# Block 0's top-k moved into its w_q products, nine weight buffers in the first phase, and a new pace in the second

## The reference

```python
x = x + mixed @ w_out                      # mixed: window attention (8 heads) and retention (8 heads) of RMSNorm(x) @ w_in
q = (h @ w_q).reshape(PEER_BLOCK, 8, 2, 128)            # h = RMSNorm(x), in blocks of 128 frames
s = einsum('thcd,hcnd->thcn', q, sub_keys)              # 16 rows of 128 scores per frame
sv, si = top_k(s, 16)
cand = sv[:, :, 0, :, None] + sv[:, :, 1, None, :]      # 8 x 256 candidates, and their indices
top_s, pos = top_k(cand, 16); expert = take(cidx, pos); g = softmax(top_s)
hid = gelu(einsum('thkd,td->thk', u_table[expert], h))
x = x + einsum('thk,thkd->td', g * hid, v_table[expert])
y = RMSNorm(x)
```

## Time and profile before

| | us |
|---|---|
| median of 3 runs | 3667.43 |
| lowest and highest | 3660.72, 3675.81 |
| profiled execution, its time | 3681.99 |
| profiled execution, its span | 3679.9 |

### The profile page before, as it was taken

How to read it: one execution, slowest core, us unless ns; L and a number is a source line. 1 busy time by engine, 2 the same in 40 slices (tenths; PEclk the granted TensorE clock), 3 DMA queues, 4 the chain that set the end, 5 groups by cost and what they waited for, 6 DMA issues and landing times.

```text
span 3679.9 us, 27703 instructions
## 1 busy us (share of the span) xinstructions
PE 1964.1 (53%) x9448; PEld 1081.0 (29%) x9448; DVE 2036.5 (55%) x4571; ACT 323.7 (9%) x778; POOL 2104.6 (57%) x2183
## 2 busy tenths in 40 slices
PE   7976615665673347655833357565723333333446
PEld 6765511543440115433601024233401000000001
DVE  2378486467539673564476853654586744443220
ACT  2211101011110010110100010101100000000000
POOL 0034345566456675566466665665576666666665
PEclk9986866886895668767956579778856555556669
DMA  6587877999999999999998999999999999999998
GB/s 222 178 294 277 308 231 290 357 399 342 358 388 364 362 350 395 399 362 395 362 385 328 360 366 394 400 364 402 346 355 370 365 374 366 366 367 376 377 365 323
DMA packets 442170, 1286.15 MB, mean 350 GB/s; under 512 B 39408, under 2 KB 157936, under 8 KB 442032
## 3 DMA queue, kind: packets, MB, share of 16 engines
q0 software_dynamic: 313344, 1140.99, 81.7%
q1 hardware_dynamic: 126224, 134.48, 11.0%
q10 hardware_dynamic: 2464, 8.91, 0.6%
HBM read 1274.50 MB, written 9.44 MB: 349 GB/s over the span
## 4 chain that ended last, share of the span: by engine, by line
POOL 22%; another core or an unknown queue 14%; DMA 12%; issue 11%; PE 8%; DVE 5%; ACT 0%; ACTq 0%; POOLq 0%; SPq 0%
POOL ring L629 22%; DMA ring<-in_peer_v_dram,v_idx 8%; PE ps L1255 4%; PE ps L1214 4%; DMA ring<-in_peer_u_dram,u_idx 3%; DVE ring L897 3%; DMA wbuf<-in_peer_w_q_dram 1%; DVE work L974 0%; DVE work L970 0%; PE ps L1413 0%; DVE work L979 0%; DMA out_dram<-x_v 0%; PE ps L1362 0%; DVE work L1071 0%
## 5 line engine op out<-in xcount | busy, mean ns | idle before, releaser
L897 DVE CUSTOM_DVE_ANT_0 ring<-ring,ps 128x1024 f32<-128x1024 f32 x1088 | 1302.2, 1218 | 975.5 <-DMA ring<-in_peer_u_dram,u_idx 855.4
L629 POOL DMA_INDIRECT ring<-in_peer_u_dram,u_idx x1088 | 1044.5, 960 | 1061.5 <-issue 275.9
L1214 PE MATMUL ps<-ring,spread 128*32 128x512 f32 x4352 | 876.5, 910 | 1241.3 <-DMA ring<-in_peer_v_dram,v_idx 1084.9
L629 POOL DMA_INDIRECT ring<-in_peer_v_dram,v_idx x1088 | 1058.3, 973 | 495.2 <-issue 304.1
L1255 PE MATMUL ps<-wbuf,actT 128*128 128x256 f32 (+1 forms) x2944 | 703.0, 399 | 105.9 <-issue 89.0
L1214 PEld LDWEIGHTS ps<-ring,spread 128*32 128x32 f32 x4352 | 178.1, 143 | 1833.5 <-issue 1765.7
L1255 PEld LDWEIGHTS ps<-wbuf,actT 128*128 128x128 f32 (+1 forms) x2944 | 559.6, 193 | 274.4 <-issue 174.7
L970 DVE MAX8 work<-work 128x8 f32<-128x128 f32 (+3 forms) x432 | 110.8, 322 | 129.9 <-ACT work L866 119.9
L974 DVE FIND_INDEX8 work<-work 128x8 uint32<-128x128 f32 (+3 forms) x432 | 134.0, 329 | 4.9 <-issue 4.7
L699 ACT COPY spread<-weightT 128x16 f32<-128x16 f32 x64 | 14.0, 219 | 894.8 <-remote 713.7
L897 DVE DVE_READ_ACCUMULATOR2_ANT hidden<- 128x1 f32 x1088 | 89.7, 82 | 0.2 <-issue 0.2
(11 more groups left out here) (153 smaller groups left out, 1271.8 us busy)
## 6 DMA issues: line engine op xcount, KB each, us to landing
wbuf<-in_w_in_dram SPq DMA_DIRECT2D x55, 1024.0 KB
wbuf<-in_peer_w_q_dram SPq DMA_DIRECT2D x40, 1024.0 KB
wbuf<-in_w_out_dram SPq DMA_DIRECT2D x20, 1024.0 KB
ring<-in_peer_u_dram,u_idx POOLq DMA_INDIRECT x1088
ring<-in_peer_v_dram,v_idx POOLq DMA_INDIRECT x1088
x_v<-x_scratch ACTq DMA_DIRECT2D x8, 512.0 KB
out_dram<-x_v ACTq DMA_DIRECT2D x8, 512.0 KB
x_in<-in_x_prompt_dram SPq DMA_DIRECT2D x7, 512.0 KB
```

Of the source, the lines that this page charges most:

```text
L629: pool.indirect_dma_start(ring[:, at % RING, :], None, table, bass.IndirectOffsetOnAxis(ap=idx, axis=0)).then_inc(landed[at % RING], 16)
L897: ch.put(v_.tensor_tensor_reduce(out=row, in0=row, in1=ux_ps, scale=1.0, scalar=0.0, op0=ALU.mult, op1=ALU.add, accum_out=hidden[:, k:k + ...
L1214: mm = pe.matmul(ps[j:j + 32, B_ACC + c, :], spread[:, at:at + 32], tile[:, 512 * c:512 * c + 512], start=(t % 32 == 0), stop=(t % 32 == 3 ...
```

## The change

Phase 0 gets nine weight buffers: the three of `wbuf`, two in `wide`, four in ring places 5 to 12. SyncE issues all 23 pieces of block 0 in one row, each when the piece nine before it has been used, and only then the x loads of blocks 1 and 2, then the store of block 0's x. The first half of the query transposes goes behind w_q product 4, its score products behind product 5, their copies with them; the h transposes go behind products 2 and 6. The second half's score products go between piece 0 and piece 1 of the early projection, and for block 0 both halves use banks 0 and 1. The copy of block 0's row into PSUM (`load`) moves from the list of phase 1 to ScalarE's work ahead of the copies of piece 1. TensorE's transpose of the expert numbers comes after four pieces of the early projection instead of eight. GpSimd's first gather also waits for the four query copies. `BEGUN_PEER` = 58 takes the place of 105 for phase 1, so its total is 346: the slot of norm2 and w_q rises, and all 128 U rows stand ahead of the top-k steps.

```diff
+WFIRST = 9
-    NORM, PIECE, ATTN, PEER = 6, 3.6, 55, 105
+    NORM, PIECE, ATTN, PEER, BEGUN_PEER = 6, 3.6, 55, 105, 58
...
-                            ("w_q", g * N_Q * self.PIECE), ("peer", g * self.PEER)):
+                            ("w_q", g * N_Q * self.PIECE),
+                            ("peer", g * (self.BEGUN_PEER if begun else self.PEER))):
...
+        wfirst = ([wbuf[:, i] for i in range(WRING)]
+                  + [wide[:, i * KC * WCOLS:(i + 1) * KC * WCOLS].rearrange("p (k n) -> p k n", k=KC) for i in range(2)]
+                  + [ring[:, i:i + 2, :].rearrange("p r (k n) -> p (r k) n", n=WCOLS) for i in (5, 7, 9, 11)])
...
-                m = n - WRING
+                m = n - (WRING if b0 else WFIRST)
...
@@ block.sync @@
-                    stream(blocks, range(N_IN))
+                    for n in range(PIECES):
+                        load_piece(blocks, n)
                     for b in following:
                         load_x(b)
-                    stream(blocks, range(N_IN, PIECES))
+                    sp.wait_ge(x1_ready, N_OUT)
+                    sp.dma_start(x1_dram[0, :, :], x_of[0]).then_inc(x1_stored[place(0)], 16)
                     stream(following, range(EARLY_LOADS))
@@ block.gpsimd @@
                     if b == 0 and k == 0:
                         pool.wait_ge(first_experts, 1)
                         pool.wait_ge(x1_stored[place(0)], 16)
+                        pool.wait_ge(pqT_ready, 4)
@@ block.scalar @@
-                        if b == 0 and m in early_h:
-                            h_copied(early_h[m], following[early_h[m]])
+                        if b == 0 and m == 2:
+                            h_copied(0, following[0])
+                        if b == 0 and m in (4, 7):
+                            pq_copied(b, 2 * (m // 7), P)
+                        if b == 0 and m == 5:
+                            sims_copied(b, 0, P)
+                        if b == 0 and m == 6:
+                            h_copied(1, following[1])
...
-                    if b == 0:
-                        projected(following, range(EARLY - 2))
+                    else:
+                        projected(following, range(1))
+                        sims_copied(b, 2, T)
+                        load(b)
+                        projected(following, range(1, 4))
                     th.step("peer", g, 0.85)
                     act.wait_ge(gdiff_ready, b + 1)
...
-                        projected(following, range(EARLY - 2, EARLY))
+                        projected(following, range(4, EARLY))
@@ block.vector @@
-                    dve.wait_ge(sims_ready, 4 * b + 4)
+                    dve.wait_ge(sims_ready, 4 * b + 4 if b else 2)
...
+                        if b == 0 and h0:
+                            dve.wait_ge(sims_ready, 4)
@@ block.tensor @@
-                        if b == 0 and m in early_h:
-                            h_transposed(early_h[m], following[early_h[m]], h2T_ready, 2)
+                        if b == 0 and m == 2:
+                            h_transposed(0, following[0], h2T_ready, 2)
+                        if b == 0 and m == 4:
+                            pe.wait_ge(hT_ready, 2 * (following[0] + 1))
+                            pq_transposed(b, 0, P)
+                        if b == 0 and m == 5:
+                            similar(b, 0, P)
+                        if b == 0 and m == 6:
+                            h_transposed(1, following[1], sims_ready, 2)
...
+                    else:
+                        pe.wait_ge(hT_ready, 2 * (following[1] + 1))
+                        pq_transposed(b, 2, T)
+                        project(following, grp + 1, range(1))
+                        similar(b, 2, T)
                     if b == 0:
-                        pe.wait_ge(sims_ready, 4)
-                        project(following, grp + 1, range(EARLY))
+                        project(following, grp + 1, range(1, 4))
                     th.step("peer", g, 0.95)
                     pe.wait_ge(expert_ready, 2 * b + 1)
                     transposed(0, T, lambda c: expert_f[0:T, :], 1, expert_tr)
+                    if b == 0:
+                        project(following, grp + 1, range(4, EARLY))
```

More of the change, by code:

```diff
@@ L675, in item, with load @@
                     spread_out(b, k)
[L676 to L682, removed]
+                elif kind == "load" and b:
+                    load(b)
                 elif kind == "final":
                     final(b)
+            def load(b):
+                act.wait_ge(h2_ready, b + 1)
+                if b == SAMPLE:
+                    act.wait_ge(sample_packed, 48)
+                ch.settle()
+                ch.put(copy(ux_ps, u_x[:, b % UXBUF, :]), ux_ready)
             def spread_out(v, piece):
@@ L741, in h_copied, with q_bank, pq_copied, sims_copied @@
                     ch.put(copy(act_of[b][:, 4 * i:4 * i + 4, 0:T], four(i, T)), hT_ready)
+            def q_bank(b, i):
+                return i % 2 if b == 0 else i
+            def pq_copied(b, first, T):
+                for i in (first, first + 1):
+                    act.wait_ge(pq_tr, 4 * b + i + 1)
+                    ch.put(copy(pqT[:, 4 * i:4 * i + 4, 0:T], four(q_bank(b, i), T)), pqT_ready)
+            def sims_copied(b, first, T):
+                for i in (first, first + 1):
+                    act.wait_ge(sims_done, 4 * b + i + 1)
+                    ch.put(copy(sims[0:T, 4 * i:4 * i + 4, :], four(q_bank(b, i), P)[0:T]), sims_ready)
             def projected(blocks, pieces):
@@ L860, in _ @@
                         act.wait_ge(expert_ready, 2 * b)
[L861 to L866, removed]
-                    if b == 0:
-                        projected(following, range(EARLY - 2))
+                        for i in (0, 2):
+                            pq_copied(b, i, T)
+                        for i in (0, 2):
+                            sims_copied(b, i, T)
+                    else:
+                        projected(following, range(1))
+                        sims_copied(b, 2, T)
+                        load(b)
+                        projected(following, range(1, 4))
                     th.step("peer", g, 0.85)
@@ L1234, in h_transposed, with q_bank, pq_transposed, similar @@
                     transposed(i, T, lambda c: h_nat[0:T, (4 * i + c) * P:(4 * i + c + 1) * P], 4, h_tr)
+            def q_bank(b, i):
+                return i % 2 if b == 0 else i
+            def pq_transposed(b, first, T):
+                pe.wait_ge(q_ready, N_Q * b + 2 * (first + 2) if b == 0 else N_Q * (b0 + G))
+                for i in (first, first + 1):
+                    transposed(q_bank(b, i), T, lambda c: pq_of[b][0:T, (4 * i + c) * P:(4 * i + c + 1) * P], 4, pq_tr)
+            def similar(b, first, T):
+                for i in (first, first + 1):
+                    pe.wait_ge(pqT_ready, 4 * b + (first + 2 if b == 0 else 4))
+                    for c in range(4 * i, 4 * i + 4):
+                        mm = pe.matmul(ps[0:T, q_bank(b, i), (c % 4) * P:(c % 4 + 1) * P], pqT[:, c, 0:T],
+                                       keysT[:, c, :], start=True, stop=True)
+                    mm.then_inc(sims_done, 1)
             def project(blocks, grp, pieces):
@@ L1401, in _ @@
                     th.step("peer", g)
-                    pe.wait_ge(q_ready, N_Q * (b0 + G))
-                    pe.wait_ge(h2T_ready, 2 * (b0 + G))
-                    if b == 0:
[L1405 to L1417, removed]
-                        pe.wait_ge(sims_ready, 4)
-                        project(following, grp + 1, range(EARLY))
+                    if b:
+                        pe.wait_ge(h2T_ready, 2 * (b0 + G))
+                        pe.wait_ge(q_ready, N_Q * (b0 + G))
+                        if g:
+                            pe.wait_ge(sims_ready, 4 * b)
+                            pe.wait_ge(expertT_ready, b)
+                        for i in (0, 2):
+                            pq_transposed(b, i, T)
+                        for i in (0, 2):
+                            similar(b, i, T)
+                    else:
[3 more added lines that the diff above has]
+                        similar(b, 2, T)
+                    if b == 0:
+                        project(following, grp + 1, range(1, 4))
                     th.step("peer", g, 0.95)
```

21 lines of the change are left out of this document (15 added, 6 removed).

## The result

The changed kernel takes 3693.85 us (median of 8 runs, 3681.21 to 3700.87), the kernel before 3677.15 beside it (3660.72 to 3686.69, 8 runs). The ratio is 1.0053, 95% interval 1.0029 to 1.0076: by that ratio 19.5 us slower (the two medians differ by 16.7), where +1.4 was forecast. A second set of runs gave 1.0055 (1.0034 to 1.0077). The profiled execution took 3694.40, its span is 3692.2.

The account below looks back on a forecast made before the run. Taken as bound by transfers with DMA full, the change being worth the shift in block 2's top-k end (634.5 us): +16.8 + 11.4 + 5 + 2 - 28 - 5.8 = +1.4, so 3669 us, range 3640 to 3692.

Parts of the forecast that it names:

- part 2: Block 0's early projection: 14 products remain behind the wait for the second indices, ending 258.7 against 241.9; +16.8 us.
- part 3: Second phase: dots move ahead; +11.4 us in attention, +5 behind the norm, w_out free, empty w_q stretch not filled.
- Part 1: Block 0's top-k: starts 11.8 us earlier, at 142.8 instead of 154.6; first indices at 171.1, second at 206.7.
- +6 named as a bound: w_out: two dots and an addition fit under a product, costing nothing; up to +6 us if w_out pieces come late.
- the empty stretch of w_q: 417 to 461 us, VectorE idle: four more dots delay the twelve products there rather than overlap them.
- the gelu wait: Before block 1's top-k: VectorE waits for ScalarE's table load and gelu behind the last score copy; +2 us (0.5 to 3).
- Part 4: Block 1's top-k: 24 dots leave it while VectorE is full; -28 us.
- Part 5: Block 2's top-k: 32 gathers issued instead of 44, VectorE's 21.3 us of gaps shrink with them; -5.8 us, bounds 0 and -21.
- the rest that was costed at nothing: Nine buffers, SyncE's order with later x loads, GpSimd's wait on pq copies, TensorE's wait for score copies: no cost expected.
- weights starve: Slower rival, w_out and w_q: weights come late at 53 GB/s; +6 and +13.8, sum +21, 3689 us; chance 0.20.

Follow-up runs that it names:

- the loop in w_q: VectorE waits for each w_q product before the next slot's dots; in the changed kernel with transpose behind six pieces 0.9938, with the old pace too 0.9937.
- the kernel before with the loop: Kernel before, second phase only: VectorE waits for each w_q product before the next slot's dots, laying 33 dots along 16 products; ratio 0.9921.
- the loop in every phase: Kernel before, dots laid along the w_q products in every two-block phase, step ahead of the wait; ratio 0.9886, 3611.7 us beside 3657.6.

## Why the prediction was wrong

The forecast was no change, +1.4 us, inside 3640 to 3692; measured was 3693.9, slower by 0.53%. Of the distance to the forecast's 3669, 9.7 us are not the change's: the forecast counted from 3667.4, the median of three runs, and the kernel before took 3677.15 beside the changed one. The rest is the change's, and by the table the sum is short by 18.7 us. The step that failed is **part 2**, "14 remain behind it ... 258.7 against 241.9", sized at +16.8 and measured at +24.0, the largest of the misses (7.2 of the 18.7). Its mechanism was right, and so were its dates up to the second indices (142.8, 171.1 and 206.7 forecast; 142.75, 171.25 and 206.4 measured; that they fit to 0.3 us is in part luck, since the first of them came anywhere from 138.1 to 142.8 in the nine traces with the early top-k). It took the 14 products behind the wait at their pace of before. But part 3 of the same forecast put 14 dots ahead of the attention, and those free 14 gathers in one run beside these very products. Beside ten such TensorE stopped for 1.7 us at most (six traces), beside 14 for 4.1 to 7.2 (seven), here for 7.2, which is the whole of the term's miss. The traces give a table for the attention's date:

| | 10 early dots | 14 early dots |
|---|---|---|
| transpose behind four pieces | 257.5, 257.0 | 269.2, 269.1 |
| transpose behind six pieces | 241.9 | 255.4, 252.2 |

By these dates the order is worth 14 to 17 us and the burst 10 to 14. But block 0's first MAX8 was itself up to 4.7 us earlier in one trace than in another, with no difference in the work ahead of it. Counted from that MAX8 the table reads 117.4 and 116.8, 126.4 and 127.5; 103.9, 114.1 and 109.7: the order is worth 12 to 18 us, the burst 6 to 11, and they add within that scatter. (The kernels at 241.9 and 252.2 also have the loop in w_q, which comes later than this date, and like the one at 257.0 they have TensorE's shorter stop at the first indices.) For the total time the order's share is shown by timing: 1.0053 and 1.0055 with it, 1.0021 and 1.0017 without, 12 us or so (each pair of intervals just overlaps, the two pairs agree). The burst's is not: 1.0049 with ten dots and 1.0026 with the old pace as a whole, beside 1.0053. How much of the burst's delay survives to the end stays open.

**Part 1** held, and was worth nothing, as forecast: what block 0's top-k gains, the projection behind it gives back. **Part 3**: ten dots more up to w_out made VectorE busy for 11.4 us more, as said, and that stretch 9.7 longer. The six further dots, costed at nothing, were not free: w_out took 32.5 instead of 29.0 us for its eight products, with 2.9 us of TensorE's waiting put down to a transfer of w_out's weights, inside the +6 named as a bound, and the stretch from there to the norm 1.1 more; the four dots behind the norm cost 5.0. That the dots ahead don't fill the empty stretch of w_q was right: 44 us with some five products, then eleven. But the reason given, that the weights get only 53 GB/s beside the dots' gathers, was wrong: it is ScalarE that stands, as shown above. The queue's share beside them is the same as in the earlier trace rows, since little was asked of it here too. From a window of 416 to 460 of the changed kernel:

```profile
DMA packets 5806, 17.87 MB, mean 406 GB/s; under 512 B 539, under 2 KB 1750, under 8 KB 5804
...
q1 hardware_dynamic: 1530, 2.29, 14.0%
```

But the end of the run cost more. ScalarE's copy at 468.37 came after 11.7 us of "remote", 8 us behind the last dot:

```profile
468.37 0.65 ACT L886 COPY wide<-ps 128x256 f32<-128x256 f32 x2 [11.73 <-remote]
```

Before, its copy at 417.29 came with the end of the dots. That accounts for the +3.9 beside the gelu wait, which was 2.1 as said.

**Part 4**: -24.5 for -28. The top-k without dots holds 4.0 us of gaps, the mixed one 0.8. TensorE takes 24 V rows at its start and GpSimd issues 24 gathers in a run; that the gaps come from these is not shown. **Between the top-k's** 2.6 us were left out: TensorE has stood for 29 us when the scores of block 2 come, and the 32 score matmuls took 6.04 instead of 3.84, in their first 3 us at a granted clock of 0.5, the 1.2 GHz level.

**Part 5**: 32 gathers as counted, -7.3 for -5.8. VectorE's gaps went from 21.3 to 14.1 us. The Trainium skill ("Runtime: NRT & Kernel Launch", instruction fetch mechanics) says that the cost of fetching instructions is mostly hidden; by that the gaps would have stayed as they were. They did not in this pair of traces, but nothing in a trace shows that the gaps are fetches. Nor is the scaling by gathers shown: the kernel before with the loop has 44 gathers beside a block 2 top-k with 16.2 us of gaps, and with the loop in every phase, again with 44, the same stretch has 10.6. So the term came out near its -5.8 in part by luck.

Of the rest that was costed at nothing, all stayed there: the x loads landed in time (ScalarE read the first at 114.64, 114.30 before), w_in ran at 3.45 per product, GpSimd's new wait ended before the first indices.

The rival "weights starve" named the right direction, and its price was mostly not paid: 3.5 of its 6 us in w_out, and of its 13.8 in w_q nothing, where the weights were not what was waited for. The loss came by a way that none of the rivals had.

## What to carry to other kernels

When a queue of transfers can fill the DMA, count how many its consumer frees in one run, and look at what every other engine does in that time: the same number of dots, laid between the products, made the kernel 0.8% faster in one phase and 1.1% in all, while moving them to the front by the pace gained nothing. A low rate of a queue isn't a reason by itself. Look first whether it had more to move, and which wait the stopped engine was in. A wait that is moved ahead of work has the price of all work behind it, at the pace that this work will have then, not the one that it had in the old trace. And an edit that is harmless alone (the pace, 1.0000) has to be priced together with the other where their dates meet.

## What the runs showed of the hardware

- Beside runs of gathers of 0.52 MB each ScalarE stops without an engine or a transfer that the trace names as the reason, and TensorE with it, when both its product buffers are full. At the first indices (14 gathers) ScalarE's copies waited 12.4 to 14.4 us in all fourteen traces, and TensorE 3.6 to 8.0. At the second indices ScalarE waited 7.5 to 13.2 us, and TensorE 4.1 to 7.2, in seven traces with a run of 14; 7.7 at most, TensorE 1.7 at most, in six with a run of 10; the one trace with no gathers there has no stop. In w_q, beside 33 to 37 dots and their gathers in one run, single waits of ScalarE were 20.7 to 32.6 us. What the stop is, no run here shows. In the changed kernel no packet of an instruction queue moved inside either of block 0's two stops.
- With the gathers spread out, each issued behind a dot that waits for a product, the 16 w_q products took 64 us instead of 84, dots included, and ScalarE's longest such wait was 6.2 us in five traces.
- Block 0's first MAX8 came between 138.1 and 142.8 in nine profiled executions of the eight kernels with the early top-k, with no difference in the work ahead of it. Dates from single traces can be told apart from some 5 us on.
